# Mixer A as one block of 40 steps, with attention laid between the weight units

## The reference

```
def mixer_a(h, w_qkv, w_o, q_gain, k_gain):      # h = rms_norm(x) : [1, 256, 2048]
    qkv = h @ w_qkv                              # 2048 x 3072: 16 query, 4 key, 4 value heads of 128
    q = axial_rope(rms_norm(q, q_gain))
    k = axial_rope(rms_norm(k, k_gain))
    ...
    logits = einsum('bqkgd,bskd->bkgqs', q_blk, k) * HEAD_DIM ** -0.5
    p = softmax(logits, axis=-1)                 # each query sees all 256 keys
    o = einsum('bkgqs,bskd->bqkgd', p, v)
    return o @ w_o                               # 2048 x 2048
```

## Time and profile before

| | |
|---|---|
| median of 3 runs | 3335.1 us (3332.38 to 3336.19) |
| the profiled execution | 3335.9 us, of which 3334.1 us from the first to the last instruction |
| TensorE busy | 3287.6 us (99%) |
| VectorE, ScalarE busy | 2020.0 us (61%), 1628.7 us (49%) |
| mean granted TensorE clock | 0.997 |
| mixer A's part of the span | 0 to 298.4 us |

### The profile page before, as it was taken

How to read it: one execution, slowest core, us unless ns; L and a number is a source line. 1 busy time by engine, 2 the same in 40 slices (tenths; PEclk the granted TensorE clock), 3 DMA queues, 4 the chain that set the end, 5 groups by cost and what they waited for, 6 DMA issues and landing times. The chain is left out here.

```text
span 3334.1 us, 43109 instructions
## 1 busy us (share of the span) xinstructions
PE 3287.6 (99%) x18176; PEld 2855.2 (86%) x18176; DVE 2020.0 (61%) x2450; ACT 1628.7 (49%) x1877; POOL 0.2 (0%) x4
## 2 busy tenths in 40 slices
PE   8999999999999999999999999999999999999998
PEld 7768888888888999998888888888898888898987
DVE  6765774774665555555576567476565654664654
ACT  5554553553444444443554355355454653464653
POOL 0000000000000000000000000000000000000000
PEclk9999999999999999999999999999999999999999
DMA  6525556556556555555555555555754456754444
GB/s 222 183 79 187 189 196 208 190 193 214 189 201 197 182 186 183 181 181 180 181 189 192 195 189 190 191 190 189 245 174 136 152 167 227 232 171 139 157 162 177
DMA packets 499225, 615.54 MB, mean 185 GB/s; under 512 B 21765, under 2 KB 383391, under 8 KB 498008
## 3 DMA queue, kind: packets, MB, share of 16 engines
q1 hardware_dynamic: 495576, 606.49, 55.0%
q10 hardware_dynamic: 3456, 6.29, 0.6%
HBM read 606.39 MB, written 12.63 MB: 186 GB/s over the span
## 5 line engine op out<-in xcount | busy, mean ns | idle before, releaser
L242 DVE TENSOR_TENSOR low<-raw,high 128x2048 fp32r<-128x2048 f32 (+3 forms) x564 | 1242.7, 2204 | 891.6 <-ACT high L234 887.3
L234 ACT ACTIVATE high<-raw 128x2048 fp32r<-128x2048 f32 (+3 forms) x564 | 1041.0, 1847 | 1256.7 <-PE bank L280 608.1
L270 PE MATMUL bank<-h,high 128*128 128x512 f32 x4672 | 1124.4, 393 | 3.0 <-PEq L1699 1.0
L270 PEld LDWEIGHTS bank<-h,high 128*128 128x128 f32 x4672 | 859.8, 188 | 178.1 <-issue 9.2
L280 PEld LDWEIGHTS bank<-h,low 128*128 128x128 f32 x4672 | 599.0, 191 | 22.7
L280 PE MATMUL bank<-h,low 128*128 128x256 f32 x4672 | 606.0, 283 | 0.0
L259 PE MATMUL bank<-high,y_high 128*128 128x512 f32 x1208 | 472.2, 391 | 4.0 <-DVE hy_tmp L2758 2.3
L261 PE MATMUL bank<-high,y_low 128*128 128x512 f32 x1208 | 470.3, 389 | 0.0
L260 PE MATMUL bank<-low,y_high 128*128 128x512 f32 x1208 | 470.2, 389 | 0.0
L259 PE MATMUL bank<-high,h 128*128 128x256 f32 (+4 forms) x1112 | 361.7, 325 | 2.3 <-DVE h L519 1.3
L261 PE MATMUL bank<-high,h 128*128 128x256 f32 (+4 forms) x1112 | 354.4, 319 | 0.0
(11 more groups left out here) (282 smaller groups left out, 1886.5 us busy)
## 6 DMA issues: line engine op xcount, KB each, us to landing
raw<-in_w_up SPq DMA_DIRECT2D x176, 1024.0 KB, 5.0
raw<-in_w_down SPq DMA_DIRECT2D x88, 1024.0 KB, 5.1
raw<-in_w_in SPq DMA_DIRECT2D x84, 1024.0 KB, 5.0
raw<-in_b_w_qkv SPq DMA_DIRECT2D x72, 1024.0 KB, 5.0
raw<-in_w_out SPq DMA_DIRECT2D x32, 1024.0 KB, 5.0
raw<-in_a_w_qkv SPq DMA_DIRECT2D x24, 1024.0 KB, 5.1
raw<-in_b_w_o SPq DMA_DIRECT2D x24, 1024.0 KB, 5.1
raw<-in_a_w_o SPq DMA_DIRECT2D x16, 1024.0 KB, 5.1
```

The costliest lines, as they stand in the source:

```text
L234: act.activation(c.high[u % SPLIT][:, 0:n], c.raw[u % RAW][:, 0:n], ACT.Copy).then_inc(c.w_high, 1)
L242: dve.tensor_tensor(c.low[u % RAW][:, 0:n], c.raw[u % RAW][:, 0:n], c.high[u % SPLIT][:, 0:n].bitcast(F32), ALU.subtract).then_inc(c.w_low, 1)
L270: pe.matmul(banks[:, i, :], wh[:, k, i * P:(i + 1) * P], c.h[:, k0 + k, :, :].rearrange("p a n -> p (a n)"), start=k0 + k == 0, stop=False ...
```

## The change

The three blocks become one class `MixerA` with a single block of 40 **steps**, one weight unit each. The column groups now come as keys, values, then four groups of queries (steps 0 to 23), and the output units follow (24 to 39), ordered so that output groups 0 and 1 alternate while the last heads finish (`A_OUT`). Tables of step numbers lay the rest between the units: `A_SCORE_AT` gives the step in which each head is scored (one head a step in 16 to 23, two a step in 24 to 27); its probabilities are transposed one step later and multiplied with the values two steps later. `A_JOB_AT` gives the steps of the ten transposing jobs. In each step TensorE does the jobs, then the heads, then the unit. Scores, transposes and outputs now have one PSUM bank each (0, 1 and 2), jobs and tables share bank 3. The table loads are issued in six portions behind the unit loads of steps 3 to 8, and the tables are turned in steps 9 to 14.

At the start, SyncE issues only the identity and one of the four gain transfers ahead of x; the other three go out on ScalarE's queue, whose first function load is put ahead. Unit 0 comes in two halves and is split in halves, x group 0 likewise, and TensorE starts the first half unit before x groups 2 and 3 are transposed.

```
+A_SCORE_AT = (16, 17, 18, 19, 20, 21, 22, 23, 24, 24, 25, 25, 26, 26, 27, 27)
+A_JOB_AT = (7, 8, 15, 16, 19, 20, 23, 24, 26, 27)
...
+    def sync(self, sp):
...
+        for s in range(A_STEPS + KT):
+            load_unit(c, sp, self.u0 + s + RAW)
+            if s == 3:
+                sp.wait_ge(c.x_squared, 8)
+            if 3 <= s < 9:
+                self.tables.load(sp, s - 3, 6)
+            if s == 15:
+                self.tables.store(sp)
...
+    def tensor(self, pe):
...
+        self.enter.turn(pe, 0)
+        self.enter.turn(pe, 1)
+        pe.wait_ge(self.first_low, 1)
+        self.products(pe, 0, (0, 1))
+        pe.wait_ge(self.g_taken, 1)
+        self.enter.turn(pe, 2)
+        pe.wait_ge(c.w_low, 1)
+        self.products(pe, 0, (2, 3)).then_inc(c.w_used, 1)
...
+    def pe_jobs(self, pe, s):
...
+        if 9 <= s < 15:
+            if s == 9:
+                pe.wait_ge(self.jobs_taken, 2)
+            self.tables.turn(pe, s - 9)
...
+    def pe_heads(self, pe, s):
+        c = self.c
+        for i in range(2):
+            for n in self.heads_at(s - 1)[i:i + 1]:
+                pe.wait_ge(self.weighted, n + 1)
...
+                if n:
+                    pe.wait_ge(self.copied, n)
...
+            for n in self.heads_at(s)[i:i + 1]:
+                pe.wait_ge(self.jobs_taken, 3 + 2 * (n // 4) + n % 4 // 2)
+                if n:
+                    pe.wait_ge(self.masked, n)
...
+    def scalar(self, act):
...
+        for s in range(A_STEPS + KT):
+            self.act_jobs(act, s)
+            if s < A_STEPS + KT - 1:
+                split_high(c, act, u0 + s + AHEAD)
...
+            self.act_heads(act, s)
+            if s % 4 == 0 and 0 < s <= A_STEPS and s != 8:
+                self.act_sizes(act, s // 4 - 1)
...
+    def vector(self, dve):
...
+            for g in (0, 2, 3, 4, 5):
+                self.dve_rotate(chain, g, s - 4 * (g + 1))
+            if 9 <= s < 15:
+                self.tables.take(dve, s - 9)
+            self.dve_heads(dve, chain, s)
+            if 4 <= s < A_STEPS + KT - 1:
+                split_low(c, dve, u0 + s + AHEAD)
...
+    def dve_rotate(self, chain, g, step):
...
+        halves = {(5, 1): (0, 1)}.get((g, step), {1: (0,), 2: (1,)}.get(step, ()) if g < 5 else ())
```

More of the change, by code:

```diff
@@ L365, in bank @@
     def bank(self, g, t):
-        return self.c.bank[SUM_BANK[g] + t]
+        return self.c.bank[(LOAD_BANK if self.kind == "load" else SUM_BANK)[g] + t]
     def cols(self, t, g):
@@ L511, in high, with low @@
                 ins.then_inc(c.h_high, 1)
[L513 removed]
+    def low(self, dve, g, pair=None):
         c = self.c
[L515 removed]
+        for k in range(4) if pair is None else (2 * pair, 2 * pair + 1):
             kt = 4 * g + k
@@ L732, in load @@
+            pairs += [(self.conv_rows[:, i, tap, :], c.w["conv_w"][i, tap].rearrange("(k p) -> k p", p=P)) for tap in range(3)]
+        pairs += [(self.table[0:32, :], c.w["rel_bias"]), (self.hot, self.consts["b_hot"])]
         for layer in range(2):
@@ L1434, in _, with heads_at @@
-        @block.vector
-        def _(dve):
-            chain = Chain(dve, own)
-            def maxima(n):
+                self.sync(sp)
+            @block.scalar
+            def _(act):
+                self.scalar(act)
+            @block.vector
+            def _(dve):
+                self.vector(dve)
+            @block.tensor
+            def _(pe):
+                self.tensor(pe)
+        c.u0 += A_STEPS + KT
+    def heads_at(self, s):
+        return [n for n in range(A_HEADS) if A_SCORE_AT[n] == s]
@@ new lines, in jobs_at, with slab, rope_index, job @@
+    def jobs_at(self, s):
+        return [i for i in range(len(A_JOB_AT)) if A_JOB_AT[i] == s]
+    def slab(self, g):
+        return (self.k, self.v)[g] if g < 2 else self.q[g % 2]
+    def rope_index(self, g):
+        return max(g - 1, 0)
+    def job(self, i):
+        g, h = (i // 2 + 1 if i >= 2 else 0), 2 * (i % 2)
+        first = 4 * (g - 2) % 8 + h
+        dst = self.q_t[:, first:first + 2, :] if g else self.k_t[:, h:h + 2, :]
+        return g, (head_pieces(self.slab(g), 0, (h, h + 1)), both(dst), P ** -0.5 if g else 1.0)
@@ new lines, in act_jobs, with act_sizes @@
+    def act_jobs(self, act, s):
+        for i in self.jobs_at(s):
+            act.wait_ge(self.jobs, i + 1)
+            if i >= 6:
+                act.wait_ge(self.scored, 2 * (i - 6) + 2)
+            take_job(act, self.job(i)[1], self.c.bank[3]).then_inc(self.jobs_taken, 1)
+    def act_sizes(self, act, g):
+        r, slab = self.rope_index(g), self.slab(g)
+        act.wait_ge(self.taken, 2 * (g + 1))
+        for t in range(TB):
+            for h in range(4):
+                done = 8 * r + 4 * t + h
+                if done:
+                    act.wait_ge(self.summed, done)
+                act.activation(self.squares[:, :], slab[:, t, h * P:(h + 1) * P], ACT.Square,
+                               accum_out=self.stat[:, 0, t, r, h:h + 1]).then_inc(self.summed, 1)
+        act.wait_ge(self.summed, 8 * r + 8)
+        act.activation(self.stat[:, 1, :, r, :], self.stat[:, 0, :, r, :], ACT.Sqrt, scale=1.0 / P,
+                       bias=self.c.eps[:, 0:1]).then_inc(self.rooted, 1)
```

863 lines of the change are left out of this document (325 added, 538 removed).

## The result

The changed kernel takes **3348.45 us** (median of 6 runs, 3346.77 to 3350.36), the kernel before, on the same chip, 3333.86 (6 runs, 3332.36 to 3336.19). The ratio is 1.004, with a 95% interval of 1.003 to 1.005: 13 us by the ratio, 14.6 by the medians. The profiled execution took 3346.77, the shortest of the six, so the trace shows a little less of the loss than the medians do.

A forecast was written before the change was run, and what follows sets the result against it. TensorE, busy 99% of the span, was taken to bound the kernel. Gains of 17.0 against 5.6 + 3.6 + 7.4 + 3.7 + 5.0 gave +8.3; 3335.9 + 8.3 - 0.8 = 3343.4 us, range 3331 to 3353.

The forecast's parts named there:

- the case held likeliest: Whole kernel: all waits come about as counted, 3339 to 3349 us; chance 0.42.
- Start, 4.1: Start of mixer A: x lands sooner and the first product starts at 12.2; gain 4.1 us, from 2.5 to 5.5.
- Step 9, 5.6: First table transpose: TensorE waits for the last table loads, queued behind step 8's unit load; 5.6 us, 5.0 to 6.6.
- Steps 17 to 22, 3.6: Attention heads: new waits by ScalarE and VectorE, behind squares, root, rotation and exponentials; together 3.6 us.
- Steps 24, 25, 7.4: Waits for a shared score bank, a copy behind a split, and a reduction behind both rotation halves; 7.4 us.
- Steps 26 to 29, 3.7: Second head's transposes wait for the first's copy behind the split, then an output copy; 3.7 us.
- Clock, 5.0: TensorE's clock falls behind the waits of 5.6 and 4.5, 2.5 each; 5.0 us, between 2 and 15.
- Attention, 12.9: Attention block of mixer A: TensorE's waits there are removed; gain 12.9 us.
- The rival that the waits are hidden: Steps 17 to 29: hand-offs stay hidden, waits sum to under 3; all gone, 3326 us, faster; chance 0.09.
- that of the small loads passing the unit's data: Step 9: small loads could pass the unit's data, so no wait; 3335 us, same; chance 0.10.

The follow-up runs named there:

- Experiment 4: Changed kernel with the old start: all gain transfers on SyncE ahead of x, first products only after the third x group and whole first unit; 3353.68 us, ratio 1.0054.
- experiment 1: Changed kernel with the small tables loaded in five portions in steps 3 to 7, not six in steps 3 to 8; 3339.92 us, ratio 1.0012.
- experiment 2: Changed kernel with the five head-norm square roots on ScalarE replaced by a scaled copy, so no function load within mixer A; 3342.02 us, ratio 1.0018.
- experiment 5: Changed kernel with VectorE's rotations behind the step's attention heads from step 17 on; 3349.79 us, ratio 1.0045.
- 12: Changed kernel with tables in four portions, copy ahead of rounding, and late rotation halves in VectorE's gaps behind heads' maxima; 3325.39 us, ratio 0.9971.
- 11: Changed kernel: four table portions, late rotation halves behind heads' maxima, ScalarE's rounding behind its heads except in steps with sums of squares; 3322.31 us, ratio 0.9963.
- experiment 10: Changed kernel: four table portions, copy ahead of rounding, rotation halves of steps 17, 21 and second of 25 behind the heads; 3339.05 us, ratio 1.0012.
- experiment 3: Changed kernel with ScalarE's first copy of turned probabilities ahead of the step's rounding of a unit; 3346.22 us, ratio 1.0033.
- experiment 6: Changed kernel with tables in four portions, copy ahead of rounding, and rotations behind the heads from step 17 on; 3342.28 us, ratio 1.0018.

## Why the prediction was right

It said 3343.4 and slower by 0.25%; it is 3348.45 and 0.4%. The places and their causes were right, and the sum came out 5 short, just inside the upper end of the case held likeliest (3339 to 3349). Its terms in the trace, where mixer A is 13.0 longer and not 8.3:

- **Start, 4.1.** First product at 12.02 for 12.2, x group 1 at 10.40 for 10.3, seven or eight slow matmuls for nine or ten. Experiment 4 gives 4.4 in the trace and 4.7 in time.
- **Step 9, 5.6.** It took 7.28: the term that was most mis-sized, and the only one beyond its own bounds (5.0 to 6.6). I let the unit load's 5.1 from issue to landing stand for the small ones behind it. They were there 7.25 after the unit's issue, 4.2 after the last of their own; in experiment 1, 6.9 and 3.2. That the place in the queue is the cause is shown (experiment 1).
- **Steps 17 to 22, 3.6.** 2.95, 0 and 1.55: 4.5. The chain had it right (exponentials behind maximum behind rotation half behind root), and removing its load shortened both waits (experiment 2). I had VectorE alone end it; in the trace ScalarE's rounding, copy and second load end only 0.74 before it. So in step 18 VectorE's order alone gives back no more than 0.74 (2.21 left in experiment 5, 2.30 in 12), and both orders together leave 0.80 (11).
- **Steps 24, 25, 7.4.** 1.26, 1.95 and 4.56: 7.8. That the rotation halves make the wait for the maximum is shown: one half moved away takes 2.9 off it (experiment 10), both nearly all (11).
- **Steps 26 to 29, 3.7.** 0.90, 0.90, 1.33 and 0.61: 3.7. The rounding as cause is shown for the first two, and for 0.55 of the third (experiment 3).
- **Clock, 5.0.** About 5.4, by three falls of 1.6 to 2.1 and not two of 2.5: right in sum only, and that by luck. I took half of the stretch behind 2404, but TensorE's slow work here lasted 3.1 to 4.2 us. The third, in step 18, was only an end of my range.
- **Attention, 12.9.** What is left of the sum: 13.0 = 23.3 + 5.4 - 4.4 - G gives 11.3, 1.6 less. A head in the stream takes 2.18 (0.44 transposes, 0.87 values, 0.87 scores), close to the 2.21 that I took. The units behind small work take 5.6 to 5.8 us from their first matmul to the next work and not 5.44, but behind a score 0.2 of that is the score's own end. I haven't split it further; where the 1.6 went stays open.

The 4.7 between 13.0 and 8.3 are 3.0 of waits, 0.4 of clock and 1.6 of missing gain, less 0.3 of start. The rival that the waits are hidden fell on the squares standing behind the exponentials; that of the small loads passing the unit's data fell on 7.28. The page "ScalarE: Activation LUTs" of the Trainium skill, section "What ACT_TABLE_LOAD costs", adds a drain of 1.38 to a load of 1.28. The trace doesn't agree: in experiment 11 the exponential begins 0.01 behind the load (120.67 after 119.38 + 1.28), and leaving the loads out shortened the waits of steps 18 and 25 by 1.38 each, not by 2.66.

## What to carry over

When stages are laid between each other, ask of each operation that is queued on an engine who waits for it and what that engine would otherwise do: the last group's rotation made TensorE wait 4.6 us when it stood ahead of a head's maximum, 4.0 behind the heads, and about 1 in small waits when it stood in the gaps in which VectorE waits for ScalarE's exponentials. Small loads belong ahead of a queue's next gated load and not behind it, since the gate opens when their reader is already there. Tables and copy gave back 12 us and the orders 13 to 15, some 4 of which lie behind mixer A and aren't shown to be theirs; the change as first made, which looked like an idea that doesn't pay, was 0.8% from the version of it that does.

## What was unexpected of the hardware

- **The same wait, with and without a fall.** At step 18 the granted clock fell behind a wait of 2.22 in experiment 10 and of 2.21 in experiment 5 (0.62 over 133.5 to 137), but not behind 2.30 in experiment 12 and 2.21 in experiment 6 (1.00 over 125 to 129). The windows of 10 and of 12:

```profile
125.00:129.00 4.00, 3.95 (x13) 3.42 (x14) 3.83 (x7) 2.40 (x2) 0.00 (x0) 0.59 0.58 224
```

```profile
125.00:129.00 4.00, 3.81 (x19) 3.33 (x20) 3.93 (x9) 2.98 (x4) 0.00 (x0) 1.00 0.60 232
```

  The work ahead is nearly alike. The 3.08 of the later stage, shown with the result, does the same, though nothing near it was changed. A wait of 2 to 3 us is a risk of a fall (some 1.7 us in step 18) and not a price.
- **The clock column is blind at the start.** The profile gives a granted clock of 1.00 for 0 to 16 us, while the matmuls of 12.59 to 15.15 stand 0.43 apart, twice the 0.227 of the stream and the pace of the rows where the column shows 0.50. Here the distance between rows has to be read and not the column.
- **Small transfers are late as a group.** Transfers of 0.5 to 198 KB behind a megabyte were there 4.2 us after the last issue, though nearly all data had moved by 71.5, 1.7 before TensorE went on. In experiment 1 it was 3.2 after the last issue.
